# Sixteen diagonals of a unit made by VectorE in two operations instead of by ScalarE one at a time

## The chip, the cores and the metric

The kernel runs on one core of one Trainium2 chip. The metric is the device time of one execution in microseconds (us), lower is better, and the number that stands for a kernel is the median of its runs.

## The reference

Two model blocks follow each other on 256 latent rows (and 256 context rows) of 1024 values. All data is float32. The part that the change touches is the feed-forward layer called PEER, which the first block runs in both of its layers:

```
s = einsum('thpd,pkd->thpk', q, sub_keys)            # 8 heads, 2 x 128 sub-keys
s1, i1 = top_k(s[:, :, 0], 16);  s2, i2 = top_k(s[:, :, 1], 16)
top_s, pos = top_k(all 256 sums s1 + s2, 16)          # 16 experts per row and head
wts = softmax(top_s)
act = gelu(einsum('thkd,td->thk', u_tab[idx], xb)) * wts
out = einsum('thk,thkd->td', act, v_tab[idx])         # summed over heads and the 16 experts
```

`u_tab` and `v_tab` have 16384 rows of 1024 values each, and which rows are read depends on the data. Layer 0 does this for 512 rows (context and latent), layer 1 for the 256 latent rows. Around it stand a gated chunk MLP and a gated linear attention (first block), and stick-breaking attention, a state-space model, sparse attention and two squared-ReLU MLPs (second block).

## The kernel before

Rows are worked on in blocks of 128, one row to a partition. A **unit** is one block and one head: layer 0 has 32 units, layer 1 has 16. A unit needs 16 rows of `u_tab` and 16 of `v_tab` for each partition. Each of these is one indirect DMA issued by GpSimd (POOL) at L2357, 128 rows of 4 KB, so 512 KB; there are 1536 of them in all.

Every gathered tile goes into the ring `GR` of 13 slots in the tile BIG. The slots are handed out strictly in turn, so GpSimd can only issue a gather when the slot taken 13 gathers earlier is free. `peer` (L601) writes a pipeline of two units: at step j of 16 it gathers u row j of unit u and v row j of unit u - 1, in that order, and mixes in one step of routing for unit u + 1 and one step of other work (`rest`, `extra`, `ends`: mixers, modulation, preparing the next block, finishing the last one). All engines run this same order from in-order queues; semaphores tie them.

- `u_dot` (L1961, VectorE): waits for u row j, multiplies it with the block's input (held in PSUM) and reduces it to a column of `ACTV`. It frees the u slot.
- `activate`: after the sixteenth dot ScalarE applies gelu to `ACTV` (L1545), then VectorE multiplies with the softmax weights (L1974).
- `v_sum`: for two v rows at a time ScalarE makes two diagonals (L1552). A diagonal `dg` is `twin` (two 64x64 identities, one above the other, in a 128x64 tile) scaled in each partition by that partition's value for row i. There are six `dg` tiles in a ring, each free when TensorE has used it. TensorE then multiplies diagonals with v rows (8 matmuls of 64x64 by 64x512, L1155), adds them up in the four PSUM banks `PV` over all 8 heads of a block, and so frees both v slots.

ScalarE's queue also holds, in order, the copies of TensorE's results out of PSUM (L1491, L1502, L1509), the exponential of routing (L1531), the copies of spread rows (L1473), and the square roots of the norms (L1497). A diagonal stands behind whatever of these was written ahead of it.

```
self.v_gather(l, u - 1, j)
if j % 2:
    self.v_sum(l, u - 1, j - 1, b, h)
next(nxt, None)                 # one step of routing for unit u + 1
```

Of the kernel before, what the change touches and what calls it, by code (L numbers as in the profile page):

```python
# [8 lines left out]
ALU = mybir.AluOpType  # L9
ACT = mybir.ActivationFunctionType  # L10
# [73 lines left out]
def beats(n):  # L84
    for _ in range(n):
        yield


def together(*works):

    works = list(works)
    while works:
        for w in list(works):
            if next(w, 0) == 0:
                works.remove(w)
        yield


def run(*works):
    for _ in together(*works):  # L100
        pass
# [7 lines left out]
class Chip:  # L109


    def __init__(self, nc, A, out, ctx):
        self.A, self.out = A, out

        def sb(name, shape, dt=F32):
            return ctx.enter_context(nc.sbuf_tensor(name, shape, dt))
# [47 lines left out]
                     "b": Slots([self.SC[32 * i:32 * i + 1, 1024:2048] for i in range(4)],  # L164
                                [sem(f"end{i}_landed") for i in range(4)])}
        self.row_from, self.width = {}, {}
        self.DG = Slots([sb(f"dg{i}", [128, 64]) for i in range(6)])
        self.V16 = sb("V16", [128, 2, 16])
        self.I16 = sb("I16", [128, 2, 16], U32)
        self.I16f = sb("I16f", [128, 2, 16])  # L170
# [79 lines left out]
        return self.pe, self.act, self.dve, self.pool, self.sp  # L250

    def rings(self):
        return (self.wide, self.narrow, self.XP, self.PO, self.PV, self.W, self.BC, self.GR, self.MR, self.MP, self.LINE["a"], self.LINE["b"], self.DG,
                self.RL, self.LG, self.PT, self.UP, self.DOWN, self.RM, self.WB)

    def begin(self, final):
# [45 lines left out]
class Engine:  # L302
# [22 lines left out]
    flip = load_slab = load_one = mm = evac = norm = row_op = spatial_mm = spatial_gate = gated_add = nothing  # L325
    queries_mm = query_rows = query_flip = keys_load = route_scores = route_top = route_pairs = nothing
    route_pick = route_which = route_hot = route_index = route_weights = block_begin = hold = nothing
    activate = u_gather = v_gather = u_dot = v_sum = fold = tiles = gate_rows = gate_sums = nothing
    ctx_decay = ctx_flip = ctx_state = lat_begin = lat_decay = lat_flip = lat_scaled = lat_scores = nothing
    intra = inter = read_state = group_norm = group_scale = group_gate = state_begin = coefficients = drive = nothing  # L330
    power = local_scan = carry_scan = spread_scan = column = row_part = side_half = side_one = nothing
# [269 lines left out]
    def peer(self, l, order, late, more, close=()):  # L601
        m, A = self.m, self.m.A
        self.prepared, self.settled = set(), set()
        units = [(b, h) for b in order for h in range(8)]
        self.load_queries(l, 0)
        self.keys_load(l)
        run(self.prepare(l, order[0], 0))
        run(self.queries(l, order[0], 0, 0, True))
        run(self.route(l, 0, *units[0]), self.queries(l, order[0], 1, 0, True))
        self.barrier("peer", l)  # L610
        m.PS = m.narrow
        rest, extra, ends = self.prepare_rest(l, order, late), self.others(more), iter(())
        for u in range(len(units) + 1):
            while u + 1 < len(units) and units[u + 1][0] not in self.prepared:
                next(rest)
            nxt = self.route(l, u + 1, *units[u + 1]) if u + 1 < len(units) else iter(())
            if u:
                b, h = units[u - 1]
                if h == 0:
                    self.block_begin(l, b)  # L620
                if h == 7:
                    names = ("mod", "peer", l, 5, b), ("ln_g", l, 1, b), ("ln_b", l, 1, b)
                    self.fetch(names[0], m.mod_row(l, 5, STREAM[b]), m.mod_stored(l, 5), "b")
                    self.fetch(names[1], A["ln_g"][l, 1], (), "b")
                    self.fetch(names[2], A["ln_b"][l, 1], (), "b")
                self.activate(l, u - 1)
            if u < len(units) and units[u][1] == 0:
                self.hold(l, units[u][0], order)
            for j in range(16):
                if u < len(units):  # L630
                    self.u_gather(l, u, j)
                    self.u_dot(l, u, j, units[u][0])
                if u:
                    self.v_gather(l, u - 1, j)
                    if j % 2:
                        self.v_sum(l, u - 1, j - 1, b, h)
                next(nxt, None)
                if u == 0 and len(order) > 2:
                    next(rest, None)
                for back in (ends, rest):  # L640
                    if next(back, 0) != 0:
                        break
                else:
                    next(extra, None)
            for _ in nxt:
                pass
            if u and h == 7:
                for _ in ends:
                    pass
                ends = self.finish(l, b, *names)  # L650
                next(ends)
        if close:
            run(extra)
        run(ends, iter(close))
        run(extra)
        self.barrier("peer done", l)
        m.PS = m.wide
# [208 lines left out]
    def sb(self, b, pace):  # L866

        m, w = self.m, self.m.A["sb_ssm_w_in_2"][0]
        q, k, v, u = (("sb_in", b, n) for n in range(4))
        if b == 0:  # L870
            self.state_begin()
            self.sb_early(0)
        self.flip(("sb", b), b, m.X[:, b, :], m.dve.at("settled", 1, b))
        after = self.flipped(("sb", b), [b])
        yield from beats(pace)
        if b == 0:
            self.coefficients()
        yield from self.columns(u, self.block_of(b), m.s_u, after, pace)
        self.side_slab(q, w, 0)
        yield  # L880
        for j in range(16):
            self.drive(b, j)
            if j % 2:
                yield
        self.side_slab(k, w, 512)
        yield from together(self.state_space(b, pace), self.attention(b, q, k, v, pace))
        for c in range(4):
            self.ssm_read(b, c)
            yield
        for c in range(4):  # L890
            self.glu(b, c)
            yield
        self.sb_gate(b)
        yield from beats(pace)
        yield from self.out_and_norm(("sb_out", b), b, (m.A["ln_mix_g_2"][0], m.A["ln_mix_b_2"][0]), m.both,
                                     [m.act.at("sbo", b, 7), m.dve.at("sb gated", b)])
# [135 lines left out]
class Tensor(Engine):  # L1032
# [112 lines left out]
    def v_sum(self, l, u, j, b, h):  # L1145

        m = self.m
        pv = m.PV.of(l, b)
        self.wait_ge(m.act.at("diagonal", l, u, j + 1), m.GR.landed("v", l, u, j), m.GR.landed("v", l, u, j + 1))
        for n in range(2):  # L1150
            for i in range(2):
                row, dg = m.GR.of("v", l, u, j + i), m.DG.of(l, u, j + i)
                for r in range(2):
                    p = slice(64 * r, 64 * r + 64)
                    mm = self.e.matmul(pv[64 * i:64 * i + 64, 2 * r + n, :], dg[p, :],  # L1155
                                       row[p, n * 512:n * 512 + 512], start=h == 0 and j == 0,
                                       stop=h == 7 and j == 14)
        mm.then_inc(*self.done("sum", l, u, j))
        if h == 7 and j == 14:
            self.done.note("block sum", l, b)  # L1160
        for i in range(2):
            m.GR.free(("v", l, u, j + i), self.done.last())
            m.DG.free((l, u, j + i), self.done.last())

    def gate_rows(self, b, j, gs):
        m, use = self.m, "ctx" if b > 1 else "lat"
# [276 lines left out]
class Scalar(Engine):  # L1443
# [97 lines left out]
    def activate(self, l, u):  # L1541
        m = self.m
        av = m.ACTV[:, u % 4, :]
        self.wait_ge(m.dve.at("dot", l, u, 15))
        self.e.activation(av, av, ACT.Gelu_apprx_tanh).then_inc(*self.done("gelu", l, u))  # L1545

    def v_sum(self, l, u, j, b, h):
        m = self.m
        for i in (j, j + 1):
            dg = m.DG.take(l, u, i)  # L1550
            self.wait_ge(m.dve.at("active", l, u), m.dve.at("twin"), *m.DG.emptied(l, u, i))
            self.e.activation(dg[:, :], m.twin[:, :], ACT.Copy, scale=m.ACTV[:, u % 4, i:i + 1]).then_inc(  # L1552
                *self.done("diagonal", l, u, i))

    def fold(self, l, b, n):

# [209 lines left out]
class Vector(Engine):  # L1766
# [203 lines left out]
    def activate(self, l, u):  # L1970
        m = self.m
        av = m.ACTV[:, u % 4, :]
        self.wait_ge(m.act.at("gelu", l, u))
        self.e.tensor_tensor(av, av, m.WT[:, u % 4, :], ALU.mult).then_inc(*self.done("active", l, u))  # L1974

    def gate_rows(self, b, j, gs):
        m = self.m
# [624 lines left out]
```

## Time and profile before

| what | value |
|---|---|
| median of 3 runs | 3753.95 us |
| lowest and highest | 3736.56 and 3755.88 us |
| span of the profiled execution | 3751.8 us |
| TensorE busy | 2608.3 us, 70% |
| VectorE busy | 1998.1 us, 53% |
| GpSimd busy | 1507.8 us, 40% |
| ScalarE busy | 710.4 us, 19% |
| HBM traffic | 1152.84 MB read, 308 GB/s over the span |

No time is given for the profiled execution other than its span, from its first to its last instruction, so the span stands for it here; it is 2.1 us under the median. How to read it: the two PEER layers lie at about 175 to 1890 us (layer 0) and 2110 to 2990 us (layer 1). Between them is the latent part of the linear attention, and behind them the second block's MLPs and sparse attention.

### The profile page before, as it was taken

To read this page: it belongs to the slowest core of one execution; us is meant where nothing else is said; L and a number is where in the kernel's file an instruction comes from. 1 tells how busy PE (TensorE), PEld (TensorE's weight loads), DVE (VectorE), ACT (ScalarE), POOL (GpSimd) and SP (SyncE) were. 2 spreads that over 40 slices of the span, in tenths; PEclk is the share of its full clock that TensorE was granted. 3 is DMA by queue.
4 is the path that set the end of the run, shared out by engine and by line. 5 is a ranking of instruction groups with operands and counts; after the bars stand their busy time and mean duration, and the time that the engine had idled before them with its cause. 6 is when DMAs were issued, how large, how long until landed. Compare 5 with 4: busy or idle time off the path is not lost.

```text
span 3751.8 us, 35602 instructions
## 1 busy us (share of the span) xinstructions
PE 2608.3 (70%) x12888; PEld 1195.8 (32%) x12888; DVE 1998.1 (53%) x5016; ACT 710.4 (19%) x1775; POOL 1507.8 (40%) x1609
## 2 busy tenths in 40 slices
PE   6687766655556675655679666556654798899998
PEld 1233222111112221111144221112311385676765
DVE  0465656656657656776422476667698436221411
ACT  1121111211112311211132112112221213020300
POOL 0025555555665666566600056666466400000000
PEclk8888888788776887676679778777877899999999
DMA  8779998999998999899923489999999776667677
GB/s 316 269 275 342 342 344 326 367 402 401 365 361 320 356 363 340 320 364 361 359 100 122 149 326 384 361 364 332 348 354 334 298 260 255 219 251 249 215 255 258
DMA packets 363676, 1156.38 MB, mean 308 GB/s; under 512 B 33712, under 2 KB 33968, under 8 KB 362476
## 3 DMA queue, kind: packets, MB, share of 16 engines
q0 software_dynamic: 232144, 849.51, 60.5%
q1 hardware_dynamic: 130940, 304.36, 22.7%
q8 instruction: 102, 1.67, 0.2%
q14 instruction: 74, 0.61, 0.0%
q10 hardware_dynamic: 416, 0.23, 0.0%
HBM read 1152.84 MB, written 1.15 MB: 308 GB/s over the span
## 4 chain that ended last, share of the span: by engine, by line
PE 42%; DVE 19%; DMA 14%; issue 7%; POOL 7%; another core or an unknown queue 5%; ACT 5%; SPq 0%; DVEq 0%; ACTq 0%; POOLq 0%
PE PS L1155 10%; PE PS L1089 8%; POOL BIG L2357 7%; DVE BIG L1965 7%; PE PS L1360 6%; PE PS L1378 6%; DMA BIG<-in_p_v_dram,IDX 6%; DMA BIG<-in_p_u_dram,IDX 5%; PE PS L1254 2%; PE PS L1348 1%; PE PS L1117 1%; DVE SC L2151 1%; DMA WR<-in_w_mod_dram 1%; ACT dg L1552 1%
## 5 line engine op out<-in xcount | busy, mean ns | idle before, releaser
L1155 PE MATMUL PS<-BIG,dg 64*64 64x512 f32 x6144 | 1059.3, 823 | 849.7 <-ACT dg L1552 383.5
L2357 POOL DMA_INDIRECT BIG<-in_p_u_dram,IDX x768 | 734.5, 956 | 1163.2 <-ACT PS L1539 417.8
L1965 DVE CUSTOM_DVE_ANT_0 BIG<-BIG,PS 128x1024 f32<-128x1024 f32 x768 | 927.8, 1215 | 325.8 <-DMA BIG<-in_p_u_dram,IDX 294.3
L2357 POOL DMA_INDIRECT BIG<-in_p_v_dram,IDX x768 | 732.0, 953 | 313.7 <-issue 180.6
L1155 PEld LDWEIGHTS PS<-BIG,dg 64*64 64x64 f32 x6144 | 274.9, 172 | 1520.9 <-issue 963.4
L1089 PE MATMUL PS<-WR,HT 128*128 128x512 f32 x640 | 294.4, 614 | 9.9 <-DMA WR<-in_a_w_in_dram 6.6
L1552 ACT ACTIVATE dg<-twin,ACTV 128x64 f32<-128x64 f32 x768 | 208.0, 336 | 345.2 <-PE PS L1155 149.8
L1360 PE MATMUL PS<-HT,WR 128*128 128x128 f32 x2048 | 256.1, 285 | 5.9 <-DMA WR<-in_mlp_w_dram 5.9
L1360 PEld LDWEIGHTS PS<-HT,WR 128*128 128x128 f32 x2048 | 247.3, 200 | 15.8 <-issue 8.9
L1378 PE MATMUL PS<-WR,BIG 128*128 128x512 f32 x512 | 226.0, 596 | 0.0
L1089 PEld LDWEIGHTS PS<-WR,HT 128*128 128x128 f32 x640 | 122.3, 196 | 177.0 <-issue 167.9
L1378 PEld LDWEIGHTS PS<-WR,BIG 128*128 128x128 f32 x512 | 97.1, 192 | 117.2 <-issue 117.0
L1117 PE MATMUL PS<-WR,HT 128*128 128x512 f32 x192 | 97.4, 666 | 14.4 <-DVE HT L1793 9.2
L2392 POOL DMA_DIRECT2D BIG<-in_dsa_w_dram x20 | 15.0, 752 | 198.9 <-PE PS L1399 103.4
L1076 PE MATMUL PS<-ident,H 128*128 128x128 f32 x152 | 31.4, 369 | 86.3 <-DVE H L1835 39.5
L1887 DVE MAX8 V<-SCU 128x8 f32<-128x128 f32 x192 | 56.6, 295 | 64.1 <-ACT SCU L1523 31.9
L1787 DVE TENSOR_TENSOR MB<-MB,PS 2x512 f32<-2x512 f32 x24 | 16.2, 674 | 136.5 <-PE PS L1055 131.6
L1531 ACT ACTIVATE WT<-WT 128x16 f32<-128x16 f32 x48 | 10.3, 216 | 399.4 <-DVE WT L1951 213.1
L1254 PE MATMUL PS<-HT,BIG 128*128 128x128 f32 x576 | 73.7, 286 | 13.5 <-DMA BIG<-in_sb_ssm_w_in_dram 9.4
L1793 DVE COPY HT<-PS 128x512 f32<-128x512 f32 x28 | 19.3, 689 | 116.3 <-PE PS L1076 92.4
L1046 PE MATMUL PS<-WR,scS 128*32 128x512 f32 x384 | 60.8, 729 | 26.6 <-DMA WR<-in_w_mod_dram 26.6
L2274 DVE TENSOR_TENSOR BIG<-BIG 128x512 f32<-128x512 f32 x32 | 22.1, 690 | 101.5 <-ACT BIG L1718 101.3
(320 smaller groups left out, 2709.7 us busy)
## 6 DMA issues: line engine op xcount, KB each, us to landing
WR<-in_mlp_w_dram SPq DMA_DIRECT2D x128, 1024.0 KB
WR<-in_w_mod_dram SPq DMA_DIRECT2D x48, 1024.0 KB
WR<-in_b_w_in_dram SPq DMA_DIRECT2D x18, 1024.0 KB
WR<-in_a_w_in_dram SPq DMA_DIRECT2D x16, 1024.0 KB
WR<-in_p_w_q_dram SPq DMA_DIRECT2D x16, 1024.0 KB
BIG<-in_dsa_w_dram POOLq DMA_DIRECT2D x16, 1024.0 KB, 7.6
BIG<-in_p_u_dram,IDX POOLq DMA_INDIRECT x768
BIG<-in_p_v_dram,IDX POOLq DMA_INDIRECT x768
```

The costliest lines, as they stand in the source:

```text
L1046: mm = self.e.matmul(ps[32 * k:32 * k + 32, :], m.scS[:, k0 + k, :], w[:, k, :], start=k0 == 0, stop=k0 == 4)
L1089: mm = self.e.matmul(ps[0:p, 0:n], lhs, rhs, start=k == 0, stop=k == kts - 1)
L1117: mm = self.e.matmul(ps, self.HT_of(k, b), m.slab_of(slab, k // 4)[:, k % 4, :], start=k == 0, stop=k == 7)
L1155: mm = self.e.matmul(pv[64 * i:64 * i + 64, 2 * r + n, :], dg[p, :], row[p, n * 512:n * 512 + 512], start=h == 0 and j == 0, stop=h == 7 a ...
L1254: mm = self.e.matmul(ps[:, i * 128:(i + 1) * 128], self.side_of(slab, k)[:, i * 128:(i + 1) * 128], rhs(k), start=k == 0, stop=k == 7)
L1348: mm = self.e.matmul(ps, lhs(k), self.side_of(slab, k), start=k == 0, stop=k == 7)
L1360: mm = self.e.matmul(ps[:, j * 128:(j + 1) * 128], m.slab_of(slab, k // 4)[:, k % 4, j * 128:(j + 1) * 128], m.HT[:, k, 256:384], start=k ...
L1378: mm = self.e.matmul(ps[:, n, :], m.F[:, k + kk, :], w[:, kk, n * 512:(n + 1) * 512], start=k + kk == 0, stop=k + kk == 31)
L1552: self.e.activation(dg[:, :], m.twin[:, :], ACT.Copy, scale=m.ACTV[:, u % 4, i:i + 1]).then_inc(*self.done("diagonal", l, u, i))
L1887: e.max(top, sc).then_inc(*self.done())
L1965: self.e.tensor_tensor_reduce(row, row, xp, 1.0, 0.0, ALU.mult, ALU.add, m.ACTV[:, u % 4, j:j + 1]).then_inc(*self.done("dot", l, u, j))
L2357: self.e.indirect_dma_start(row, None, m.A[f"p_{table}"], bass.IndirectOffsetOnAxis(ap=m.IDX[:, u % 4, j:j + 1], axis=0)).then_inc(*m.GR.l ...
```

## The change

VectorE makes the diagonals. The ring of six tiles becomes one tile `DG` of 16 diagonals. VectorE writes it in two operations of eight diagonals each (128x512 values): the product of `twin`, repeated eight times, and eight columns of `ACTV`, each repeated 64 times. The first half is made right after `activate`, the second half at step 3 of the 16, after the fourth dot and ahead of the fourth v gather in the written order. Each half waits until the previous unit's last sum that reads it is done on TensorE: sum 6 for the first, sum 14, the unit's last, for the second. It also waits for VectorE's own last write. TensorE's sums wait for one of the two halves. ScalarE's part of `v_sum` is gone. To make room in SBUF, the space set aside for GpSimd's DMA descriptors is given as 8192 bytes of each partition; before, the argument was left at its default.

```diff
-        self.DG = Slots([sb(f"dg{i}", [128, 64]) for i in range(6)])
+        self.DG = sb("DG", [128, 16, 64])
...
                 self.activate(l, u - 1)
+                self.diagonals(l, u - 1, 0)
...
                 if u:
+                    if j == 3:
+                        self.diagonals(l, u - 1, 1)
                     self.v_gather(l, u - 1, j)
...
-        self.wait_ge(m.act.at("diagonal", l, u, j + 1), m.GR.landed("v", l, u, j), m.GR.landed("v", l, u, j + 1))
+        self.wait_ge(m.dve.at("diagonals", l, u, j // 8), m.GR.landed("v", l, u, j), m.GR.landed("v", l, u, j + 1))
...
-                row, dg = m.GR.of("v", l, u, j + i), m.DG.of(l, u, j + i)
+                row, dg = m.GR.of("v", l, u, j + i), m.DG[:, j + i, :]
...
-            m.DG.free((l, u, j + i), self.done.last())
...
-    def v_sum(self, l, u, j, b, h):
-        m = self.m
-        for i in (j, j + 1):
-            dg = m.DG.take(l, u, i)
-            self.wait_ge(m.dve.at("active", l, u), m.dve.at("twin"), *m.DG.emptied(l, u, i))
-            self.e.activation(dg[:, :], m.twin[:, :], ACT.Copy, scale=m.ACTV[:, u % 4, i:i + 1]).then_inc(
-                *self.done("diagonal", l, u, i))
...
+    def diagonals(self, l, u, half):
+
+        m, js = self.m, slice(8 * half, 8 * half + 8)
+        if u:
+            self.wait_ge(m.pe.at("sum", l, u - 1, 8 * half + 6))
+        elif l:
+            self.wait_ge(m.pe.at("sum", 0, 31, 8 * half + 6))
+        self.wait_ge(self.done.last())
+        self.e.tensor_tensor(m.DG[:, js, :], m.twin[:, :].unsqueeze(1).to_broadcast([128, 8, 64]),
+                             m.ACTV[:, u % 4, js].unsqueeze(2).to_broadcast([128, 8, 64]), ALU.mult).then_inc(
+            *self.done("diagonals", l, u, half))
...
-    nc = _bacc.Bacc("TRN2", target_bir_lowering=False, num_devices=1)
+    nc = _bacc.Bacc("TRN2", target_bir_lowering=False, num_devices=1, dynamic_dma_scratch_size=8192)
```

## Rows read from the trace of the kernel before

**Rows 1.** The page: busy slices of the DMA engines, and the chain by engine.

```profile
DMA  8779998999998999899923489999999776667677
...
PE 42%; DVE 19%; DMA 14%; issue 7%; POOL 7%; another core or an unknown queue 5%; ACT 5%; SPq 0%; DVEq 0%; ACTq 0%; POOLq 0%
```

**Rows 2.** The page's costliest groups: the PEER loop's own instructions.

```profile
L1155 PE MATMUL PS<-BIG,dg 64*64 64x512 f32 x6144 | 1059.3, 823 | 849.7 <-ACT dg L1552 383.5
L2357 POOL DMA_INDIRECT BIG<-in_p_u_dram,IDX x768 | 734.5, 956 | 1163.2 <-ACT PS L1539 417.8
L1965 DVE CUSTOM_DVE_ANT_0 BIG<-BIG,PS 128x1024 f32<-128x1024 f32 x768 | 927.8, 1215 | 325.8 <-DMA BIG<-in_p_u_dram,IDX 294.3
...
L1552 ACT ACTIVATE dg<-twin,ACTV 128x64 f32<-128x64 f32 x768 | 208.0, 336 | 345.2 <-PE PS L1155 149.8
```

**Rows 3.** Windows by stage: busy us of each engine, granted clock, DMA share, GB/s.

```profile
300.00:700.00 400.00, 273.26 (x1284) 99.34 (x1276) 240.16 (x555) 68.29 (x183) 216.03 (x225) 0.85 0.92 342
700.00:1100.00 400.00, 232.58 (x1234) 59.10 (x1234) 249.50 (x585) 76.07 (x202) 234.96 (x250) 0.75 1.00 380
1100.00:1600.00 500.00, 323.36 (x1596) 107.79 (x1596) 327.62 (x765) 121.74 (x308) 302.86 (x321) 0.77 0.93 341
1600.00:1870.00 270.00, 151.36 (x777) 40.22 (x781) 160.38 (x362) 40.55 (x125) 175.25 (x187) 0.69 0.97 362
2190.00:2600.00 410.00, 243.76 (x1178) 69.59 (x1176) 273.38 (x634) 79.14 (x213) 259.95 (x275) 0.74 0.98 370
2600.00:2950.00 350.00, 203.11 (x1246) 91.15 (x1250) 270.15 (x885) 79.45 (x222) 195.00 (x202) 0.79 0.91 338
```

**Rows 4.** Waits of TensorE and GpSimd: us in total, times, longest.

```profile
PE PS L1155 <- ACT dg L1552: 383.5, 129, 11.9
PE PS L1155 <- DMA BIG<-in_p_v_dram,IDX: 355.8, 129, 6.3
...
POOL BIG L2357 <- PE PS L1155: 374.6, 127, 10.8
```

**Rows 5.** Waits at 300 to 700, 1100 to 1600, 2600 to 2950, 1600 to 1870.

```profile
PE PS L1155 <- ACT dg L1552: 65.7, 23, 6.9
...
PE PS L1155 <- ACT dg L1552: 120.2, 38, 7.0
...
PE PS L1155 <- ACT dg L1552: 99.2, 26, 11.9
...
PE PS L1155 <- ACT dg L1552: 12.9, 4, 5.2
```

**Rows 6.** Timeline at 585 to 600 us, in order of time.

```profile
585.43 3.60 PE L1117 MATMUL PS<-WR,HT 128*128 128x512 f32 x8
...
592.60 0.60 ACT L1502 ACTIVATE SC<-PS 128x512 f32<-128x512 f32 x1 [12.63 <-remote]
...
594.72 1.05 ACT L1552 ACTIVATE dg<-twin,ACTV 128x64 f32<-128x64 f32 x4
594.85 0.16 DVE L1957 RECIPROCAL sums<-sums 128x1 f32<-128x1 f32 x1 [12.47 <-ACT WT L1531]
...
595.35 5.24 PE L1155 MATMUL PS<-BIG,dg 64*64 64x512 f32 x28 [6.31 <-ACT dg L1552]
...
599.34 0.93 POOL L2357 DMA_INDIRECT BIG<-in_p_u_dram,IDX  x1 [7.88 <-PE PS L1155]
```

**Rows 7.** Groups at 300 to 2200 us: a VectorE product with repeated inputs.

```profile
L1934 DVE TENSOR_TENSOR OH<-OH,I16f 128x512 f32<-128x512 f32 x31 | 21.5, 694 | 1.1
```

**Rows 8.** Window at 2850 to 2900 us, VectorE's densest: the third pair of figures is VectorE's.

```profile
2850.00:2900.00 50.00, 26.37 (x146) 7.14 (x142) 45.42 (x143) 9.12 (x24) 32.08 (x33) 0.70 0.95 346
```

**Rows 9.** Timeline: gathers beside VectorE products, and one undisturbed gather.

```profile
1551.14 1.80 POOL L2357 DMA_INDIRECT BIG<-in_p_u_dram,IDX  x1 [2.10 <-PE PS L1155]
...
1654.18 0.69 DVE L1934 TENSOR_TENSOR OH<-OH,I16f 128x512 f32<-128x512 f32 x1
1654.60 1.08 POOL L2357 DMA_INDIRECT BIG<-in_p_u_dram,IDX  x1 [0.30 <-issue]
...
1655.98 0.94 POOL L2357 DMA_INDIRECT BIG<-in_p_v_dram,IDX  x1 [0.30 <-issue]
```

**Rows 10.** The page: the queue of GpSimd's DMAs.

```profile
q0 software_dynamic: 232144, 849.51, 60.5%
```

More of the change, by code:

```diff
@@ L252, in rings @@
     def rings(self):
-        return (self.wide, self.narrow, self.XP, self.PO, self.PV, self.W, self.BC, self.GR, self.MR, self.MP, self.LINE["a"], self.LINE["b"], self.DG,
+        return (self.wide, self.narrow, self.XP, self.PO, self.PV, self.W, self.BC, self.GR, self.MR, self.MP, self.LINE["a"], self.LINE["b"],
                 self.RL, self.LG, self.PT, self.UP, self.DOWN, self.RM, self.WB)
@@ L327 @@
     route_pick = route_which = route_hot = route_index = route_weights = block_begin = hold = nothing
-    activate = u_gather = v_gather = u_dot = v_sum = fold = tiles = gate_rows = gate_sums = nothing
+    activate = diagonals = u_gather = v_gather = u_dot = v_sum = fold = tiles = gate_rows = gate_sums = nothing
     ctx_decay = ctx_flip = ctx_state = lat_begin = lat_decay = lat_flip = lat_scaled = lat_scores = nothing
```

## The prediction

> **What bounds the kernel now.** I read the page first, the busy slices ahead of the chain of waits [rows 1]. The chain gives TensorE 42%, VectorE 19% and the DMAs 14%, which looks like a kernel bound by TensorE. But in nearly all slices of the two PEER layers the DMA engines are at 9 tenths. The reader is to see that the chain there follows whichever engine handed over last, while the DMA engines are what is full. The groups say the same [rows 2]: TensorE's sums have 849.7 us of idle time in front of them, the dots 325.8 us, and GpSimd's u gathers 1163.2 us. No compute engine of the loop is full.
>
> So I cut the PEER layers into stages and read the windows [rows 3]. At 700 to 1100 us the DMA share is 1.00, at 1600 to 1870 it is 0.97 with 362 GB/s, at 2190 to 2600 it is 0.98. A gather of 512 KB (524,288 bytes) takes 1.45 us at 362 GB/s. GpSimd could issue one every 1.24 us (0.94 us and 0.30 us between, [rows 9]), so it is not the limit. In the three other stages the share is lower: 0.92, 0.93 and 0.91. Only there is DMA time to be won.
>
> Then the waits. TensorE's sums wait 383.5 us for diagonals and 355.8 us for v rows, and GpSimd waits 374.6 us for sums to free slots of the ring [rows 4]. By stage [rows 5] the wait for diagonals is 65.7, 120.2 and 99.2 us in the three stages with DMA time to win, and 12.9 us in the stage at 0.97. So the waits for diagonals are where DMA time is lost. That is a coincidence of places so far and not yet a cause.
>
> The timeline at 585 to 600 us shows the cause, and its limit [rows 6]. TensorE ends a product of the next block's queries (L1117) at 589.03 us. ScalarE has waited 12.63 us to copy it. Diagonals stand behind this copy and behind the exponential, so they are made at 594.72 us and the sums start at 595.35 us, after 6.31 us of idle time, while GpSimd has stopped for 7.88 us for their slots. But VectorE too has stood still for 12.47 us, for the exponential behind the same copy. Its u slots are in the same ring. Without diagonals in the way the v slots come free at once, and the u slots do not.
>
> **The change part by part.** *Removed:* 768 operations of ScalarE, 208.0 us busy [rows 2]. ScalarE is not full, so this alone is worth nothing; what counts is the wait that goes with it. An upper bound of the gain is what the three stages lack to the clean stage at 1600 to 1870. By the share that is 400 x (1 - 0.92/0.97) = 20.6 us, 500 x (1 - 0.93/0.97) = 20.6 us and 350 x (1 - 0.91/0.97) = 21.6 us, 63 us in all. By the rate it is 400 x (1 - 342/362) = 22.1, 500 x (1 - 341/362) = 29.0 and 350 x (1 - 338/362) = 23.2, 74 us in all [rows 3]. The lower bound is nothing: if each stall has a second holder, as at 595 us, the DMAs stay as they are. I take half of the larger bound, 37 us, because in the one stall that I read to its end one of two holders goes. The 383.5 us of waiting are no measure of the gain: 285.1 us of them lie in the three stages [rows 5], against the 74 us that the DMAs lack there, and the other 98 us lie mostly where the DMAs are full.
>
> *Added on VectorE:* two products of 128x512 in each of 48 units. The nearest row is another product of the same size with a repeated input, 694 ns [rows 7]. With about 0.05 us to the wait on VectorE's own last write that is 1.5 us a unit and 72 us in all. It is hidden where VectorE would wait for u rows anyway (294.3 us, [rows 2]); in the stages with full DMAs it costs nothing. Where VectorE is dense it may not be: at 2850 to 2900 us it is busy 45.4 of 50 us [rows 8], and a unit takes about that long. The stage from 2600 to 2950 has 202 GpSimd operations, 6.3 units, so the cost is between 0 and 9.5 us. I take 3 us, since 4.6 us in 50 are still idle, and more than 1.5.
>
> *The start of a unit's sums.* Before, ScalarE's first pair and TensorE's start came about as far behind `activate` as one product of 694 ns will now. I take nothing, and 5 us (0.1 us in each unit) as the worst.
>
> *The new waits.* The first half waits for a sum that lies more than half a unit back in the ring of 13 slots, and is free. The second half waits for the previous unit's last sum. Behind it in VectorE's queue stand the dots of rows 4 to 15, a routing step for each, and side work; GpSimd waits for the dots to free slots, TensorE for scores and evacuations. Between the last v gather of the old unit and the fourth u gather of the new one lie 7 gathers, 7 x 1.45 = 10 us. So TensorE must be more than 10 us late with its last sum before VectorE stands still. With the ring full that far, GpSimd is blocked by the old v slot already, and VectorE can lack only one or two dots. I take nothing; the other bound is the slower rival below.
>
> *GpSimd beside VectorE.* A gather issued in the middle of a product of two SBUF tiles took 1.08 us, one beside a longer product 1.80 us, an undisturbed one 0.94 us [rows 9]. So a new product may cost GpSimd 0.14 us, 96 of them 13 us, and by the longest row 0.86 us each, 83 us. GpSimd has 0.21 us to spare at every gather (1.45 less 1.24), so I take nothing of it. The Trainium skill speaks against this change here: its page "SBUF — State Buffer", section "Who interferes with whom", says that a VectorE instruction with two SBUF inputs shuts out a GpSimd instruction that reads SBUF, for the whole instruction. The trace agrees in kind, but with less than a product's length at 1654 us. By that rule, with a full product of waiting each time and no slack to take it, the sum would be 67 us higher and the change a loss; it is among the rivals.
>
> *The smaller space for descriptors.* The trace shows 232,144 packets on GpSimd's queue [rows 10], about 144 for a gather and so 9 for each of 16 DMA engines. With 13 gathers under way that is 117 for an engine. Nothing in the trace shows how many the space holds; I take no cost, and keep the far bound as a rival.
>
> **The sum.** 3751.8 - 37 + 3 = 3717.8 us for the span. The median of the runs is 2.1 us above the span, so 3720 us.
>
> **The rivals.** *More: every stall goes.* The three stages come up to 362 GB/s. For it: TensorE has 285 us of waiting for diagonals in them [rows 5], four times the 74 us. Against: VectorE held by the same copy [rows 6]. 74 - 3 = 71 us, 3683 us; with the first 100 us of gathers also helped, some 8 us more, 3675 us.
>
> *No change that can be measured.* The second holder keeps every stall: ScalarE's copies still wait for TensorE's products, VectorE for ScalarE's exponential, and the ring fills with u rows. For it: 12.47 us on VectorE against 6.31 us on TensorE at the same place [rows 6]. Then some 10 us are won, less 3: about 3747 us.
>
> *Slower: VectorE tied to TensorE.* The wait at step 3 stops VectorE whenever TensorE is over 10 us late. TensorE's longest runs of other products, and the longest wait of GpSimd for a sum (10.8 us, [rows 4]), reach that. If it happens in every fourth unit (12 units) at 5 us, VectorE's added work is uncovered as well (9.5 us), and the gain is only 20 us, the result is 3754 + 60 + 9.5 - 20 = 3803 us. It decides from about one unit in ten. Against it: the same lateness already blocks GpSimd.
>
> *Slower: the descriptors.* If the halved space held back gathers so that the clean stages fell to the worst share seen, 0.91 for 0.97 [rows 3], the 2330 us of the six stages would grow by 6.6%, 154 us: 3874 us at the least gain of 34 us.
>
> *Slower: GpSimd held by the new products.* If each of the 96 products stopped a gather for its own length and GpSimd had no slack, 96 x 0.694 = 67 us [rows 7], 3787 us. Against it: 0.14 us and not 0.69 beside the nearest product [rows 9].
>
> **How the numbers follow.** A measurement of this kernel tells about 0.5%, 19 us, from no change. The forecast 3720 us has a chance of 0.44 (own range 3700 to 3740); every stall goes 0.16; no change 0.27; VectorE tied to TensorE 0.08; descriptors 0.03, GpSimd held 0.02. The range 3672 to 3760 us takes in the forecast, the other two on the fast side and the no-change case, and leaves out the slower ones and a little of either end. Faster by over 0.5% (under 3735 us) are nearly all of the first two and a bit of the third: 0.58. Within 0.5%: 0.30. Slower: 0.12.
>
> **What the profile after would show.** TensorE's sums wait for diagonals of VectorE for less than 60 us in place of 383.5; ScalarE's busy time falls from 710 to 502 us and VectorE's rises by 67. GpSimd's wait for sums falls from 374.6 us to about 200. The DMA share in the three stages rises to 0.94 to 0.96, and nothing moves at 700 to 1100 and 1600 to 1870 us. VectorE's wait for TensorE in front of the new products is under 20 us. The prediction is wrong if the DMA share stays at 0.92 with the waits for diagonals gone (a second holder), if VectorE waits long in front of the second half, or if gathers take over 1 us in the mean.

## The result, and the profile after

The kernel after takes 3655.5 us (median of 4 runs, 3654.9 to 3658.3) against 3751.0 us before, a ratio of 0.9753 with a 95% interval of 0.9725 to 0.9781. It is 95 us faster. 34 us were forecast, and 3672 us was the low end of the range.

The page of the kernel after: the busy slices of the DMA engines, the chain by engine, and the loop's groups.

```profile
DMA  8789999999999999999822599998999786667577
...
PE 39%; DVE 21%; DMA 20%; POOL 8%; issue 7%; another core or an unknown queue 3%; ACT 2%; SPq 0%; DVEq 0%; ACTq 0%; POOLq 0%
...
L1158 PE MATMUL PS<-BIG,DG 64*64 64x512 f32 x6144 | 1057.6, 814 | 674.0 <-DMA BIG<-in_p_v_dram,IDX 500.4
L2363 POOL DMA_INDIRECT BIG<-in_p_u_dram,IDX x768 | 735.1, 957 | 1021.4 <-ACT SCU L1525 242.5
L1959 DVE CUSTOM_DVE_ANT_0 BIG<-BIG,PS 128x1024 f32<-128x1024 f32 x768 | 927.9, 1215 | 312.7 <-DMA BIG<-in_p_u_dram,IDX 272.9
L2363 POOL DMA_INDIRECT BIG<-in_p_v_dram,IDX x768 | 738.6, 962 | 345.7 <-issue 180.4
```

The last line has this counterpart on the page of the kernel before:

```profile
L2357 POOL DMA_INDIRECT BIG<-in_p_v_dram,IDX x768 | 732.0, 953 | 313.7 <-issue 180.6
```

Against [rows 1, 2] the reader is to see three things. ScalarE has nearly left the chain (5% to 2%) and the DMAs have a larger share of it (14% to 20%). The idle time in front of the sums fell by 176 us, and what ends most of it is now v rows that land. GpSimd's time for a gather has hardly changed: 957 ns in the mean for a u row (956 before) and 962 for a v row (953 before), 7 us in all.

The waits of the kernel after.

```profile
PE PS L1158 <- DMA BIG<-in_p_v_dram,IDX: 500.4, 195, 9.6
...
PE PS L1158 <- DVE DG L1978: 34.9, 12, 7.4
...
POOL BIG L2363 <- PE PS L1158: 223.8, 100, 6.6
```

Against [rows 4] the wait for diagonals went from 383.5 to 34.9 us and GpSimd's wait for sums from 374.6 to 223.8 us.

To compare stages, both kernels have to be cut at the same work and not at the same time. The six windows run from the activation of unit 0 to that of units 8, 15, 24 and 31, and from unit 32 to 40 and 47. First the kernel before (busy us of TensorE, its weight loads, VectorE, ScalarE, GpSimd; clock, DMA share, GB/s):

```profile
258.00:723.00 465.00, 320.29 (x1472) 114.79 (x1472) 285.90 (x653) 87.45 (x220) 245.28 (x256) 0.85 0.90 335
723.00:1071.00 348.00, 202.28 (x1081) 50.93 (x1080) 218.98 (x513) 62.59 (x172) 202.48 (x214) 0.76 1.00 381
1071.00:1537.00 466.00, 298.25 (x1474) 100.14 (x1474) 297.29 (x699) 110.62 (x279) 286.08 (x303) 0.77 0.94 347
1537.00:1857.00 320.00, 181.29 (x921) 48.58 (x924) 208.66 (x476) 54.03 (x158) 204.00 (x216) 0.69 0.94 351
2198.00:2579.00 381.00, 224.11 (x1108) 63.55 (x1108) 246.48 (x577) 73.57 (x200) 240.11 (x254) 0.74 0.98 371
2579.00:2963.00 384.00, 230.09 (x1356) 99.39 (x1357) 295.40 (x939) 86.06 (x236) 217.83 (x226) 0.79 0.91 341
```

The same six windows of the kernel after:

```profile
262.00:678.00 416.00, 315.03 (x1472) 113.44 (x1472) 297.90 (x670) 56.23 (x93) 246.26 (x256) 0.86 0.97 371
678.00:1023.00 345.00, 205.10 (x1081) 51.46 (x1080) 227.67 (x525) 33.27 (x57) 204.32 (x214) 0.76 1.01 388
1023.00:1468.00 445.00, 295.69 (x1474) 100.72 (x1474) 310.55 (x718) 75.94 (x136) 287.58 (x304) 0.78 0.97 363
1468.00:1784.00 316.00, 186.64 (x922) 50.07 (x924) 215.35 (x490) 25.82 (x47) 206.85 (x217) 0.70 0.96 357
2122.00:2497.00 375.00, 222.18 (x1108) 63.45 (x1108) 256.87 (x591) 40.90 (x70) 244.73 (x256) 0.75 0.99 380
2497.00:2862.00 365.00, 238.69 (x1358) 102.29 (x1358) 304.96 (x953) 59.63 (x125) 217.92 (x226) 0.76 0.95 358
```

The stages give 49, 3, 21, 4, 6 and 19 us, 102 us in all (2364 to 2262 us). The two spans differ by 98 us, so outside the stages some 4 us are lost. 89 of the 102 us lie in the first, third and last stage, the ones that were named, with the DMA share rising from 0.90 to 0.97, 0.94 to 0.97 and 0.91 to 0.95. What was wrong is how much they would give.

Last, the place in the kernel after that answers to the stall of [rows 6], in order of time:

```profile
551.47 7.13 PE L1120 MATMUL PS<-WR,HT 128*128 128x512 f32 x16
...
558.53 5.76 PE L1158 MATMUL PS<-BIG,DG 64*64 64x512 f32 x32
...
563.25 0.60 ACT L1504 ACTIVATE SC<-PS 128x512 f32<-128x512 f32 x1 [14.30 <-remote]
563.64 0.94 POOL L2363 DMA_INDIRECT BIG<-in_p_u_dram,IDX  x1 [2.74 <-remote]
...
565.50 0.17 DVE L1951 RECIPROCAL sums<-sums 128x1 f32<-128x1 f32 x1 [10.94 <-issue]
```

The query product ends and the sums start with no idle time; before, 6.31 us lay between them. VectorE still stands still for 10.94 us behind the same copy and exponential. GpSimd now stops for 2.74 us and not for 7.88. The second holder is still there, and GpSimd stops for little of it.

### The profile page after: what moved, and what is told of

Read it like the earlier page. It is cut to its first block, busy times and chain, and to the rows that moved or that the text cites. A ratio compares the mean times of both kernels' runs of the same rounds, so it can differ in the third digit from the quotient of the medians.

```text
span 3653.6 us, 35023 instructions
## 1 busy us (share of the span) xinstructions
PE 2616.1 (72%) x12888; PEld 1202.7 (33%) x12888; DVE 2061.5 (56%) x5112; ACT 518.2 (14%) x1007; POOL 1516.7 (42%) x1609
## 4 chain that ended last, share of the span: by engine, by line
PE 39%; DVE 21%; DMA 20%; POOL 8%; issue 7%; another core or an unknown queue 3%; ACT 2%; SPq 0%; DVEq 0%; ACTq 0%; POOLq 0%
DMA BIG<-in_p_v_dram,IDX 12%; POOL BIG L2363 8%; PE PS L1158 8%; DVE BIG L1959 8%; PE PS L1092 7%; PE PS L1380 6%; PE PS L1362 6%; DMA BIG<-in_p_u_dram,IDX 4%; PE PS L1256 2%; PE PS L1350 2%; DMA WR<-in_w_mod_dram 1%; PE PS L1120 1%; DVE SC L2157 1%; DVE I L1883 1%
## 5 line engine op out<-in xcount | busy, mean ns | idle before, releaser
L1158 PE MATMUL PS<-BIG,DG 64*64 64x512 f32 x6144 | 1057.6, 814 | 674.0 <-DMA BIG<-in_p_v_dram,IDX 500.4
L1158 PEld LDWEIGHTS PS<-BIG,DG 64*64 64x64 f32 x6144 | 274.4, 168 | 1342.3 <-issue 1220.1
L1256 PEld LDWEIGHTS PS<-HT,BIG 128*128 128x128 f32 x576 | 70.8, 202 | 17.6 <-issue 9.2
```

What stands on the lines that cost most here:

```text
L1256: mm = self.e.matmul(ps[:, i * 128:(i + 1) * 128], self.side_of(slab, k)[:, i * 128:(i + 1) * 128], rhs(k), start=k == 0, stop=k == 7)
```

## The experiments

The runs came out on chips of two kinds, told apart by the kernel before itself: 3748 to 3751 us with gathers at some 360 GB/s in a clean stage, and 3564 to 3572 us with 409 GB/s (1600 to 1700 us). Each group of experiments has its own runs of the kernel before on its chip, so ratios are compared, and medians only between runs on the same kind. "Slower chip" and "faster chip" mean this below. No chip served two groups, so it is not shown that the chip makes the difference and not, say, its state or other load at that time. Most ratios in the expectations were set for the slower chip. On the faster one they are to be read against 0.9883, which is what the kernel after has there (e17).

**e1, only the descriptor space** (faster chip), the kernel before with

```diff
-target_bir_lowering=False, num_devices=1)
+target_bir_lowering=False, num_devices=1, dynamic_dma_scratch_size=8192)
```

> The kernel before with only the space for DMA descriptors given as 8192 bytes. Theory (the gain of 95 us comes from the sums no longer standing behind ScalarE's queue): no change, ratio 0.997 to 1.003. Rival (the moved or smaller space is itself worth something): ratio under 0.995.

Measured: 0.9994 (0.9982 to 1.0006). It is worth nothing and costs nothing.

**e2, sixteen tiles, same maker, same places** (faster chip), the kernel before with that and

```diff
-        self.DG = Slots([sb(f"dg{i}", [128, 64]) for i in range(6)])
+        self.DG = Slots([sb(f"dg{i}", [128, 64]) for i in range(16)])
```

> The kernel before with 16 tiles dg in place of 6 (and the descriptor space of the change), diagonals still made by ScalarE one by one in front of each sum. Theory (place in ScalarE's queue): what delays a diagonal is what stands ahead of it, not a missing free tile, so little changes: ratio 0.992 to 1.002, TensorE's wait for diagonals still over 300 us. Rival (room): six tiles let ScalarE run only three sums ahead, with 16 most of the gain comes, ratio under 0.985, and the 150 us that ScalarE's diagonals wait for TensorE disappear.

Measured: 0.9998 (0.9983 to 1.0013), with 312.5 us of waiting for diagonals. Room is not what they lacked.

**e3 and e16, ScalarE makes them early** (faster chip, twice). The kernel after, with `diagonals` moved to ScalarE:

```diff
+        for i in range(8 * half, 8 * half + 8):
+            self.e.activation(m.DG[:, i, :], m.twin[:, :], ACT.Copy, scale=m.ACTV[:, u % 4, i:i + 1]).then_inc(
+                *self.done("diagonals", l, u, half))
```

> The kernel after with its order and its tile DG, but ScalarE makes the diagonals, 8 at the unit's start and 8 at step 3, 16 operations of some 270 ns. Theory (it is the place in the order that counts, not the engine): most of the gain, ratio 0.975 to 0.985, a few us lost because the first sums wait for 8 operations (2.2 us) in place of one product. Rival (it counts that ScalarE is rid of 208 us, or that VectorE is the less blocked queue): ratio over 0.99.

> ScalarE makes all diagonals early, at the change's places in the order. Theory (it is the place in the order that counts): most of the gain on either kind of chip, ratio 0.975 to 0.985 on the slower one. Rival (ScalarE still holds them behind its copies at step 0 and step 3): 0.985 to 0.995.

Measured: 0.9873 (0.9856 to 0.9889) and 0.9852 (0.9833 to 0.9871), 3523.4 and 3518.3 us. The kernel after itself is at 0.9883 on such a chip (below). So with all 768 operations still on ScalarE, at the change's places, the whole gain of that chip is there. On the slower chip this was not measured.

**e4, VectorE makes them at the old places** (faster chip), two at a time in front of each sum:

```diff
                     if j % 2:
+                        self.diagonals(l, u - 1, j // 2)
                         self.v_sum(l, u - 1, j - 1, b, h)
```

> VectorE makes the diagonals two at a time (one product of 128x128) in front of each sum, at the place where ScalarE made them. Theory (place): VectorE's queue at that place holds the dots, which wait for u rows, so sums wait again, and 8 operations of about 0.3 us a unit cost 115 us of VectorE; a part of the gain only, ratio 0.980 to 0.995. Rival (any queue but ScalarE's will do): the whole gain, ratio 0.973 to 0.979.

Measured: 1.0443 (1.0422 to 1.0464), 3727.5 us. Both expectations failed; it is far slower than the kernel before. Its waits:

```profile
PE PS L1156 <- DVE DG L1976: 774.6, 279, 8.9
...
POOL BIG L2361 <- PE PS L1156: 507.4, 201, 11.5
```

A pair now stands behind the dot of the same step, which waits for a u row whose gather is written only just ahead of it. Each sum so waits for rows it does not need, and v slots stay taken. The engine is the one of the change and the operation of the same kind. What differs is the place, and with it the number of operations: 384 of 295 ns, 113 us of VectorE, against 67 us for the 96 of the change. By e6 below, where 67 us more of VectorE cost some 13 us, these 46 us are a small part. Between this and the early places lie 5.7% on the same kind of chip, some 200 us.

**e5 and e15, no diagonals at all** (faster chip, twice). Every v row enters the sums with weight one, so the experts' activations are left out of them; the calls of `diagonals` go, and

```diff
-                row, dg = m.GR.of("v", l, u, j + i), m.DG[:, j + i, :]
+                row, dg = m.GR.of("v", l, u, j + i), m.twin
```

> The kernel after without diagonals: the sums multiply the v rows with twin, so each row is added with weight one and the experts' activations are left out of the sums. It shows what diagonals cost at all. Theory (VectorE's new work is hidden, the waits on it are short): at most 15 us below the kernel after, ratio to before 0.971 to 0.976. Rival (VectorE's 67 us are partly on the path): 30 us and more below, ratio under 0.968.

> The kernel after without diagonals (sums multiply with twin, activations left out of the sums), beside the other two. If the chip is the slower one: what is left to win is under 15 us, ratio 0.970 to 0.975. It also shows whether a chip with slower gathers makes the diagonals dearer in general.

Measured: 0.9836 both times (0.9802 to 0.9870, 0.9814 to 0.9858), 3512.7 and 3508.0 us, 13 and 18 us under the kernel after on another such chip (e17), and 12 and 16 us under the variants e8 and e14 beside them, which are as fast as the kernel after. That is all that making diagonals costs there. Both runs fell on the faster chip, so the question on the slower one has no answer.

**e6, the products twice** (faster chip): each of the two products is made two times in a row.

> The kernel after with each of the two products made twice, one after the other: 67 us more of VectorE's busy time. Theory (hidden but in the dense stages): 3 to 15 us above the kernel after, ratio 0.976 to 0.980. Rival (on the path, at full price): 50 us and more above, ratio over 0.988.

Measured: 0.9901 (0.9870 to 0.9932), 3538.0 us. That is 12 us above the kernel after on another such chip, where the two intervals overlap, and 13 to 15 us above e8 and e7 on the same chip, whose runs all lie below the runs of this one. So 67 us of VectorE's work cost some 13 us, a fifth; the prediction had taken 3 us of 72, with 9.5 as the far bound.

**e7, the second half at step 0** (faster chip):

```diff
-                    if j == 3:
+                    if j == 0:
```

> The kernel after with the second half made at step 0 in place of step 3, so VectorE waits for the previous unit's last sum only one gather after it. Theory (the slower rival of the prediction is real in kind, step 3 is what hides it): VectorE stands still for TensorE in most units, ratio 0.980 to 0.995, and that wait shows over 100 us in the profile. Rival (GpSimd is blocked by the same slot anyway, so it costs nothing): ratio 0.974 to 0.977.

Measured: 0.9859 (0.9827 to 0.9890), 3523.1 us, no slower than the kernel after on such a chip. The rival holds, and the theory, which wanted over 100 us of waiting, does not. Who waited for sums in this kernel (us, times):

```profile
  DVE DG L1978: 13.9, 13
```

VectorE waits 13.9 us in 13 places. Even one gather behind the last v row VectorE hardly has to wait for the last sum, and nothing is lost.

**e8, two buffers, one product of 128x1024** (faster chip):

```diff
-        self.DG = sb("DG", [128, 16, 64])
+        self.DG = sb("DG", [128, 32, 64])
...
-            self.wait_ge(m.pe.at("sum", l, u - 1, 8 * half + 6))
+            self.wait_ge(m.pe.at("sum", l, u - 2, 14))
```

> Two buffers of 16 diagonals, all 16 of a unit made by one product of 128x1024 (about 1.23 us) at its start; it waits for the last sum of the unit before the previous one, which is long done. Theory: one operation less and no wait for the last sum, so 0 to 10 us below the kernel after, ratio 0.972 to 0.976. Rival (the longer first product delays the first sum and the next dot where slots are short): 3 to 15 us above it.

Measured: 0.9864 (0.9833 to 0.9895), 3524.9 us, the same as the kernel after. The product took 1225 ns, and nothing of the saved operation or wait shows.

**e9 and e17, the kernel after once more, on either kind of chip.**

> The kernel after, unchanged, beside the other experiments' kind of chip. On a chip whose gathers run at 409 GB/s (the kernel before at 3570 us) the ring absorbs more of each stall: ratio 0.984 to 0.988. On one at 362 GB/s (3751 us) the ratio is 0.9753 again.

> The kernel after, unchanged, for a comparison on one chip. If the chip is the one with faster gathers (the kernel before at 3570 us): ratio 0.984 to 0.988, beside 0.9836 without diagonals, 0.9852 to 0.9873 with diagonals made early by ScalarE and 0.9873 with the later copy. If it is the slower one: 0.9753 again.

Measured: 0.9747 (0.9712 to 0.9782), 3645.4 us, on the slower chip; 0.9883 (0.9863 to 0.9903), 3525.6 us, on the faster. So the same change gains 95 and 103 us on the one (by the medians of the first result and of this one) and 38 us on the other. The windows of the last, cut at the same units as above, and behind them those of the kernel with only the descriptor space, which stands for the kernel before on such a chip:

```profile
262.00:671.00 409.00, 309.36 (x1472) 112.29 (x1472) 298.09 (x670) 56.63 (x95) 249.62 (x256) 0.87 0.98 378
...
1004.00:1407.00 403.00, 293.80 (x1474) 101.17 (x1474) 310.96 (x718) 76.50 (x137) 283.62 (x300) 0.80 1.01 396
...
2381.00:2738.00 357.00, 228.12 (x1358) 98.14 (x1358) 305.13 (x955) 59.68 (x125) 218.61 (x225) 0.78 0.96 365
```

```profile
258.00:685.00 427.00, 309.83 (x1472) 111.18 (x1472) 286.55 (x654) 88.03 (x222) 247.02 (x256) 0.88 0.95 362
...
1018.00:1435.00 417.00, 284.64 (x1474) 96.57 (x1474) 298.78 (x701) 111.16 (x280) 283.78 (x299) 0.81 0.99 383
...
2417.00:2772.00 355.00, 230.96 (x1355) 98.14 (x1356) 295.24 (x939) 86.10 (x238) 218.41 (x225) 0.79 0.96 366
```

The first, third and last stage give 18, 14 and -2 us there, against 49, 21 and 19 us. The DMA engines had less to win: shares of 0.95, 0.99 and 0.96 in place of 0.90, 0.94 and 0.91.

**e10 and e11, ten slots in place of thirteen** (slower chip), in the kernel before and in the kernel after:

```diff
+        NR = 10
-        self.GR = Slots([GRt[:, i, :] for i in range(NG)], [sem(f"row{i}_gathered") for i in range(NG)])
+        self.GR = Slots([GRt[:, i, :] for i in range(NR)], [sem(f"row{i}_gathered") for i in range(NR)])
```

> The kernel before with 10 slots of gathered rows in place of 13. Theory (a stall of the sums costs what the ring does not absorb): clearly slower, ratio 1.02 to 1.06, and GpSimd's wait for sums grows. Rival (the ring's depth does not matter, the DMA engines are the limit everywhere): under 1.01.

> The kernel after with 10 slots in place of 13. Theory (the change shortens the time that a v slot stays taken, so it is worth more where there are fewer slots): it loses less to the missing slots than the kernel before does, and is 3 to 5% faster than that one with 10 slots. Rival (the gain comes from elsewhere, such as a less busy ScalarE): the gain stays what it was with 13 slots. A third: with 10 slots VectorE's wait for the last sum bites, and the gain shrinks.

Measured: 1.0095 (1.0061 to 1.0129), 3784.7 us, and 0.9861 (0.9828 to 0.9895), 3692.6 us. The kernel before loses 37 us to the missing slots and the one after loses 47. Between the two with 10 slots lie 92 us, between the two with 13 103 us. The kernel before was expected to lose 2 to 6% and lost 1%, and its GpSimd waited no longer for sums (376.3 us against 374.6). The theory that the change is worth what the ring fails to absorb has fallen, and so has its use as an explanation of the two chips.

**e12, half by VectorE, half by ScalarE** (slower chip): `diagonals(0)` as in the change, `diagonals(1)` as eight operations of ScalarE at step 3.

> The kernel after with its first half made by VectorE and its second half by ScalarE, eight operations at step 3. VectorE is rid of 33 us and of the wait for the last sum. Theory (both are hidden where they stand): within 10 us of the kernel after. Rival (they cost): 10 to 30 us below it, near the kernel without diagonals.

Measured: 0.9747 (0.9709 to 0.9784), 3653.0 us. The kernel after beside it has 0.9747 and 3645.4 us, and the runs of both spread over 3640 to 3657 us, so no difference is shown. On the slower chip too it does not matter which of the two engines makes the second half, so long as it is early.

**e13 and e14, the copy of the query products two steps later** (faster chip), in the kernel before and in the kernel after. This is the copy that held both diagonals and VectorE in [rows 6].

```diff
-        self.query_rows(l, b, n)
-        yield from beats(4)
+        yield from beats(2)
+        self.query_rows(l, b, n)
+        yield from beats(2)
```

> The kernel before with ScalarE's copy of a query product (L1502) written two steps later, so that diagonals and the exponential of routing no longer stand behind it. Both holders of the stall in the prediction's timeline go. If diagonals behind that copy are a main part of the first stage's loss, ratio 0.985 to 0.995; if not, over 0.997.

> The kernel after with the same later copy: the diagonals are away already, so only VectorE's wait for the exponential behind the copy (the second holder of the prediction) goes. The prediction's step (the second holder keeps half of each stall): 15 us and more below the kernel after, ratio 0.965 to 0.971 on the slower chip. Theory now (u rows catch up out of the ring, the second holder costs next to nothing): within 6 us of the kernel after, ratio 0.973 to 0.977.

Measured: 0.9996 (0.9984 to 1.0008) and 0.9873 (0.9855 to 0.9891), 3565.8 and 3524.4 us. In the kernel after, taking the second holder away gives nothing (3525.6 us without the edit). In the kernel before, taking both away gives nothing either. But little was there to take: VectorE's waits for the exponential, in e17 and in e14,

```profile
DVE sums L1951 <- ACT WT L1533: 21.1, 4, 13.6
...
DVE sums L1952 <- ACT WT L1534: 14.4, 3, 13.6
```

The 13.6 us lie at 236 us, ahead of the loop, in both. What the edit takes away is one wait of 6.8 us at 557 us. The copy also held few diagonals on this chip: by the timeline of e1 it stands ahead of them at 8 of 136 waits, with 11 us. The stall that I had read to its end was a clear one, and a rare one.

**e18, the exponential of routing one step later** (faster chip), in the kernel before:

```diff
         self.route_index(l, u)
         yield
+        self.route_exp(l, u)
+        yield
...
-    def route_index(self, l, u):
+    def route_exp(self, l, u):
```

> The kernel before with ScalarE's exponential of routing (L1531) written one step later, when VectorE's logits are nearly always there. In the trace of the kernel before the waits of sums for diagonals fall most often behind this exponential (about 72 us in 14 places). Theory (diagonals are late because of what stands ahead of them in ScalarE's queue, the exponential that waits for VectorE first of all): a part of the gain, ratio 0.990 to 0.997. Rival (no single holder counts, another takes its place): over 0.997.

Measured: 0.9943 (0.9923 to 0.9964), 3545.7 us against 3563.8 us. The waits in this kernel, and last the wait for diagonals of the kernel before on such a chip (e1):

```profile
PE PS L1158 <- DMA BIG<-in_p_v_dram,IDX: 485.3, 201, 5.8
...
PE PS L1158 <- ACT dg L1555: 241.7, 118, 8.6
...
PE PS L1155 <- ACT dg L1552: 313.1, 136, 12.1
```

By the timelines, an exponential that waits for VectorE's logits stands ahead of the diagonals at 22 of these waits, with 106 us, in e1, and at 6, with 27 us, here. One instruction of ScalarE written one step later (VectorE's use of its result moves along by a step), with diagonals still made one by one at their old places, gives 18 of the 38 us that the change gives on such a chip. The exponential waits for VectorE's logits, and the diagonals stood behind it.

## Why the prediction was wrong

**What bounds the kernel** was right: DMA time, lost in three stages, and the waits for diagonals as what loses it. The stages with full DMAs gave 3, 4 and 6 us.

**The step that failed is "I take half of the larger bound, 37 us".** The three stages gave 89 us, and all six 102 us. Two things in it were wrong.

The half rested on one stall and on a second holder seen in it. That holder is nearly alone in the kernel before:

```profile
DVE sums L1957 <- ACT WT L1531: 30.9, 6, 13.5
```

VectorE waits six times for the exponential. 13.5 us of that lie at 231 us, ahead of the loop, 12.47 us are the stall that was read, and the other four waits make 5 us. So a second holder could not keep half of what 129 waits for diagonals cost. Where it does hold, the profile after shows VectorE standing still for 10.94 us while GpSimd stops for 2.74 us. Slots come free in turn, and the one in front was a v slot; the dots then catch up at 1.2 us each. e14 takes the holder away and wins nothing. No share of the bound was to be given to it. Nor was the diagonals' side of the stall typical: e13 takes its cause away in the kernel before and wins nothing. The largest single holder of diagonals was the exponential of routing waiting for VectorE's logits (e18, half of the gain on the faster chip). In the timeline of the kernel before it stands ahead of some 15 waits with 70 to 80 of the 383.5 us, by how one tells holders apart; the copy of the query products accounts for some 20 us, and the rest is spread over many. A count of the holders over all 129 waits was to be had before the prediction, and one stall took its place.

The bound itself was too low for the first stage. I took 362 GB/s, from a stage with gathers alone, as the ceiling everywhere. It is none: the stage at 700 to 1100 us stood at 380 GB/s in [rows 3], and within it the kernel before has these two stretches, both with gathers alone:

```profile
910.00:940.00 30.00, 15.32 (x94) 4.26 (x86) 20.38 (x44) 3.24 (x10) 20.41 (x23) 0.83 1.03 410
940.00:1000.00 60.00, 34.66 (x178) 9.19 (x178) 40.53 (x103) 11.77 (x34) 38.18 (x41) 0.68 0.99 363
```

At 300 to 700 us, a stage that loads weights as well, the kernel after moves 382:

```profile
300.00:700.00 400.00, 298.24 (x1408) 104.88 (x1407) 282.59 (x637) 50.64 (x87) 238.48 (x249) 0.83 0.99 382
```

With that as the ceiling, an estimate made after the fact, the stage's bound is 400 x (1 - 342/382) = 42 us in place of 22, and the three are 94 us in place of 74. Of the prediction's cases "every stall goes" came nearest, and its 3675 us was 20 us high. It had 74 + 8 us in the three stages, where 89 came, and nothing in the stages with full DMAs, where 3, 4 and 6 us came. In the third and last stage 21 and 19 us came of bounds of 29 and 23, so there not every stall went.

**The other terms.** *VectorE's products* took 692 ns in the median and 696 in the mean (694 forecast). Doubling them cost some 13 us on the faster chip where 3 were taken for the first pair; with none at all 12 to 18 us are won, which holds all of the diagonals' cost. So the term was too small by some 10 us, in the direction against the error above. *The start of a unit's sums* lies in that figure. *The new waits* cost nothing, as forecast: VectorE's new products have 10.2 us of idle time ahead of them in all, and with the half at step 0 there are 13.9 us of waiting for sums. *GpSimd beside VectorE* cost little: u and v gathers took 957 and 962 ns against 956 and 953, 7 us over 96 products, or 0.07 us for each. With the products doubled (e6) they took 967 and 977 ns. The prediction read the Trainium skill ("SBUF — State Buffer", section "Who interferes with whom") as a rule against the change, with a rival of 67 us. The same section says that a `tensor_tensor` was not seen to stall DMAs, and infers as the reason that descriptor generation needs the write interface of the shared ports, while such a product takes only the read interface. The trace agrees that there is no stall of a product's length: 0.07 us and not 0.69. *The descriptor space* cost nothing (e1).

**The profile forecast**: waits for diagonals under 60 us (34.9 measured), GpSimd's wait for sums about 200 (223.8), ScalarE 502 us busy (518.2), VectorE 67 us more (63.4), DMA share of 0.94 to 0.96 in the three stages (0.97, 0.97 and 0.95).

**Engine or place.** The prediction spoke of VectorE taking over. The runs show that the engine is not it. ScalarE at the early places gains as much (e3, e16, and e12 for a half on the slower chip), VectorE at the old places loses 4.4% (e4). What counts is that the diagonals of a sum are written ahead of everything that waits for later rows and for routing. For all 16 diagonals on ScalarE this is shown on the faster chip only.

**What stays open** is why the slower chip gains 95 to 103 us and the faster one 38. In the kernel before the DMA engines are idle more on the slower one in all three stages. The depth of the ring does not explain it (e10, e11), and no run changed the rate of the gathers alone. Nor is it known why the gathers on the slower chip run at 410 GB/s for a while and then at 363, as shown above. What delayed the diagonals is shown by an experiment for the faster chip only (e18), where it is half of the gain; what made up the other half was not taken apart.

## What to carry to other kernels

A small operation that needs little and is needed by many belongs at the first place in the written order where its inputs are there, and not in front of its user: in an in-order queue it inherits every wait ahead of it. Which engine does it matters less; the same diagonals on the same VectorE were 5.7% apart between two places, a small part of it for the greater number of operations. When the gain of taking a wait away is sized, count what stands behind all of its occurrences, and look through the whole trace for a higher rate before one stage's rate is taken as the ceiling. One stall that is read to its end shows a mechanism, not its share.

## What the runs showed of the hardware

The same program ran at 3751 us and at 3564 us on different chips. From 1600 to 1700 us, where only gathers run, the rate is 362 GB/s in the kernel before on the slower one and 409 GB/s in e1 and e17. A gain measured on one of them (2.5%) was 1.2% on the other. On the slower chip too gathers alone ran at 410 GB/s for 30 us (910 to 940 us of the kernel before), right behind the last weight loads of that stage, and then at 363. With 67 us of additional VectorE products with both inputs in SBUF, GpSimd's 1536 gathers took 7 us more.
